# One more 2 MB home for expert weights, a late weight tile in another home, value weights loaded later, and copies shared by two engines

## The reference

```
block 1:  h = rmsnorm(x);  proj = h @ w_in                        # ten projections
          y_a = bidirectional gated linear attention (8 heads of 128), group norm, gate
          y_b = gelu(u) * spatial mix(layernorm(gelu(v))) * silu(g)
          x = rmsnorm(x + (sig(ma) * (y_a @ pa) + sig(mb) * (y_b @ pb)) @ w_out)
block 2:  pool mixer + sparse attention (8 heads of 64; an index with 8 heads, rotary turned,
          scores all keys and the 256 best are kept)               # "mid" and "sparse attention"
          x = x + cross attention to 256 memory tokens, 4 heads of 128
          x = x + mixture of 32 experts (1024 -> 256 -> 1024), two chosen per token
```

## Time and profile before

| | us |
|---|---|
| median of 3 runs (1450.04 to 1450.48) | 1450.24 |
| the profiled execution | 1448.69 |
| its span | 1446.8 |
| TensorE busy in it | 1366.7 (94%) |
| VectorE, ScalarE, GpSimd busy | 850.2, 426.3, 186.0 |
| bytes moved | 249.56 MB, mean 172 GB/s |

### The profile page before, as it was taken

One profiled execution on the slowest core, in us unless ns is written; L12 is line 12 of the kernel. 1 busy time (PEld: TensorE's weight loads), 2 busy tenths in 40 slices (PEclk: granted clock), 3 DMA queues, 4 the chain that ended last, 5 costly groups with the idle time before them and its releaser, 6 DMA issues. The chain is left out here.

```text
span 1446.8 us, 16453 instructions
## 1 busy us (share of the span) xinstructions
PE 1366.7 (94%) x5920; PEld 891.8 (62%) x5920; DVE 850.2 (59%) x1661; ACT 426.3 (29%) x718; POOL 186.0 (13%) x246
## 2 busy tenths in 40 slices
PE   7999999999999899999999999999899798999876
PEld 3577686887887668888887434445485445333322
DVE  5587787888888747877476459745573414222111
ACT  2434444544454215101112233133312421000000
POOL 0120212222210100000000026200000001222221
PEclk9999999999999999999999999999999999999999
DMA  8574657778752443222233333011213658999997
GB/s 322 124 175 154 130 134 179 167 182 188 169 133 78 90 159 129 87 106 88 102 131 117 88 91 106 22 51 46 88 58 137 257 190 320 400 407 404 413 407 272
DMA packets 65009, 249.56 MB, mean 172 GB/s; under 512 B 10464, under 2 KB 12128, under 8 KB 58144
## 3 DMA queue, kind: packets, MB, share of 16 engines
q1 hardware_dynamic: 43232, 207.57, 38.7%
q0 software_dynamic: 19008, 34.62, 13.3%
q10 hardware_dynamic: 2688, 6.29, 1.1%
HBM read 228.13 MB, written 12.58 MB: 166 GB/s over the span
## 5 line engine op out<-in xcount | busy, mean ns | idle before, releaser
L3474 PE MATMUL moe_banks<-weight_slots,moe_room 128*64 128x512 f32 x400 | 93.4, 617 | 10.3 <-DMA weight_slots<-in_w_gu 7.8
L659 PE MATMUL gla_proj<-hT,weight_slots 128*128 128x512 f32 x224 | 98.4, 593 | 1.9 <-DVE hT L1155 1.9
L2219 PE MATMUL mid_p_proj<-hT,weight_slots 128*128 128x512 f32 x208 | 92.1, 595 | 1.8 <-PEq L226 1.8
L3631 DVE SCALAR_TENSOR_TENSOR moe_room<-moe_banks,moe_kept,moe_room 128x256 f32<-128x256 f32 x16 | 7.7, 484 | 130.3 <-ACT moe_room L3586 130.3
L589 PE MATMUL gla_proj<-hT,weight_slots 128*128 128x256 f32 x320 | 77.2, 381 | 0.0
L844 ACT ACTIVATE gla_level_decay<-gla_level_decay 128x1024 f32<-128x1024 f32 x56 | 59.2, 1058 | 51.8 <-DVE gla_level_decay L1024 51.1
L659 PEld LDWEIGHTS gla_proj<-hT,weight_slots 128*128 128x128 f32 x224 | 41.6, 190 | 50.6 <-issue 49.8
L2219 PEld LDWEIGHTS mid_p_proj<-hT,weight_slots 128*128 128x128 f32 x208 | 39.0, 190 | 51.7 <-issue 51.6
L3474 PEld LDWEIGHTS moe_banks<-weight_slots,moe_room 128*64 128x64 f32 x400 | 29.8, 141 | 65.8 <-issue 54.7
L589 PEld LDWEIGHTS gla_proj<-hT,weight_slots 128*128 128x128 f32 x320 | 59.7, 192 | 10.5 <-issue 3.3
L589 PE MATMUL gla_proj<-weight_slots 128*128 128x256 f32 x272 | 64.6, 380 | 0.6 <-ACT weight_slots L790 0.6
(11 more groups left out here) (540 smaller groups left out, 2907.2 us busy)
## 6 DMA issues: line engine op xcount, KB each, us to landing
weight_slots<-in_w_gu SPq DMA_DIRECT2D x25, 2048.0 KB, 23.7
weight_slots<-in_w_gla SPq DMA_DIRECT2D x40, 512.0 KB, 4.2
weight_slots<-in_w_dn SPq DMA_DIRECT2D x10, 2048.0 KB, 34.7
weight_slots<-in_w_merge SPq DMA_DIRECT2D x32, 512.0 KB, 4.7
gla_w_sums<-in_w_gla SPq DMA_DIRECT2D x42, 256.0 KB, 4.7
gla_w_sums<-weight_slots POOLq DMA_DIRECT2D x40, 256.0 KB, 4.1
weight_slots<-in_w_out SPq DMA_DIRECT2D x16, 512.0 KB, 4.4
gla_w_sums<-in_w_gla POOLq DMA_DIRECT2D x28, 256.0 KB, 6.4
```

The costliest lines, as they stand in the source:

```text
L659: last = nc.tensor.matmul(pj[:, n % 2, :], lhsT, rhs, start=(k == 0), stop=(k == KT - 1))
L2219: last = nc.tensor.matmul(pw[:, n % 2, :], a, b, start=(k == 0), stop=(k == KT - 1))
L3474: last = nc.tensor.matmul(pG[rows, e, :], hgT[:, k, rows], core.as_gate_up(at[k // 4])[:, x, k % 4, :], start=(k == 0), stop=(k == KT - 1))
L3631: nc.vector.scalar_tensor_tensor(out=hid[:, e], in0=pG[:, e, FF:2 * FF], scalar=rs2[:, e, 1:2], in1=sa[:, e], op0=ALU.mult, op1=ALU.mult). ...
```

## The change

It has four parts. `PLACES` becomes 12, with a new 2 MB tensor `weight_slots_5` (`W5`) as home 11; part 11 is issued in the cross stage behind part 9. To fit, `rs_final` is allocated with the tensors that end with the mixers. The pair `(FILL, 5)` gets slots 11 and 3, and its second tile is issued after `("y", (QG, 7))`. In the mid stage the turned copy of the last index query is issued before the value weights, and the separate wait for the projection goes, as the copy's own wait covers it. In the cross stage ScalarE copies bank 0 and VectorE bank 1, each with its own semaphore, and the value product waits for each half by itself.

```diff
-PAIR_SLOTS = [(9, 10)] * 5 + [(11, 4)]
+PAIR_SLOTS = [(9, 10)] * 5 + [(11, 3)]
...
-PLACES = 11
+PLACES = 12
...
-        return (self.W3[:], quarters(self.xT), quarters(self.hT), self.W4[:], quarters(self.x_rows))[i - 6]
+        return (self.W3[:], quarters(self.xT), quarters(self.hT), self.W4[:], quarters(self.x_rows), self.W5[:])[i - 6]
...
                         if j == V_ and head < HEADS:
                             load_values(head)
-                        elif j == V_:
-                            load_tile((FILL, 5), 1)
-                        else:
+                        elif j < V_:
                             load_tile((j // 2, 1), j % 2)
...
                         elif kind == "y" and m[0] == FB:
                             load_sums((FILL, 5))
+                        elif kind == "y":
+                            load_tile((FILL, 5), 1)
...
                 turn_index(3, 2)
-                sp.wait_ge(proj_done, done_by(QI + 3))
+                turn_index(4, 3)
                 sp.dma_start(wv, dram["w_v2"].rearrange("p (k c) -> p k c", c=T)).then_inc(core.w_in[0], 16)
-                turn_index(4, 3)
...
                 sp.wait_ge(zn_done, 4)
                 core.load_part(sp, 9)
+                core.load_part(sp, 11)
...
                         if h:
-                            pe.wait_ge(t_out, MB * (h - 1) + c + 1)
+                            pe.wait_ge((t_out, t_out2)[c], h)
...
                 def values(h):
-                    pe.wait_ge(t_out, MB * (h + 1))
                     if h:
                         pe.wait_ge(y_out, h)
                     for c in range(MB):
+                        pe.wait_ge((t_out, t_out2)[c], h + 1)
...
-                    for c in range(MB):
-                        act.wait_ge(t_done, MB * h + c + 1)
-                        nc.scalar.copy(prT[:, h % 2, c], pT[:, c, :]).then_inc(t_out, 1)
+                    act.wait_ge(t_done, MB * h + 1)
+                    nc.scalar.copy(prT[:, h % 2, 0], pT[:, 0, :]).then_inc(t_out, 1)
...
+                def copy_second(h):
+                    if h >= 2:
+                        dve.wait_ge(o_done, h - 1)
+                    dve.wait_ge(t_done, MB * h + 2)
+                    nc.vector.tensor_copy(prT[:, h % 2, 1], pT[:, 1, :]).then_inc(t_out2, 1)
...
                 top(1)
                 probs(1)
                 normed(3)
+                copy_second(0)
                 top(2)
                 store(0)
                 probs(2)
+                copy_second(1)
                 top(3)
                 store(1)
                 probs(3)
+                copy_second(2)
                 store(2)
+                copy_second(3)
                 store(3)
...
-        rs1 = ctx.enter_context(nc.sbuf_tensor("rs_final", [P, T], F32))
...
+        rs1 = mixer.enter_context(nc.sbuf_tensor("rs_final", [P, T], F32))
...
+            core.W5 = sb("weight_slots_5", [P, 4, KT * P])
```

More of the change, by code:

```diff
@@ L1198, in gla_stage @@
         core.w_n[j] += 16 * HEADS
-    for slot, times in zip((4, 5, 9, 10, 11), (1, 2, 6, 6, 3)):
+    for slot, times in zip((3, 5, 9, 10, 11), (1, 2, 6, 6, 3)):
         core.w_n[slot] += 16 * times
@@ L2438, in cross_stage @@
                                           "turned", "turned_out", "o_done", "y_out", "dve_chain", "act_chain"))
-        h_ready = core.sem("h_ready")
+        h_ready, t_out2 = core.sem("h_ready"), core.sem("cr_turned_out_second")
         w0 = list(core.w_n)
```

## The result

| | before | changed |
|---|---|---|
| median of the runs | 1448.73 us (9 runs) | 1437.95 us (9 runs) |
| ratio to before, 95% interval | | 0.9938 [0.9923, 0.9952] |
| the same comparison once more, another chip session | 1447.20 us | 1438.56 us, 0.9940 [0.9922, 0.9957] |
| span of the profiled execution | 1446.8 us | 1436.6 us |

0.9938 of 1448.73 is 9.0 us less (7.0 to 11.2); the prediction had 8.7 less, 1441.5 as a median. It started from 1450.24, the median of the first three runs; the ratio taken from there gives 1441.2. The changed kernel's own median, 1437.95, lies just under the lower end of the range, 1438.0, because the nine runs of the kernel before have a lower median than its first three. The spans of the two profiled executions differ by 10.2 us.

A forecast was written before the change was run, and what follows sets the result against it. TensorE's pace bounds the early stages, the expert-weight bytes left when transfer engines fill bound the last hundred microseconds; -5.2 - 1.6 - 2.3 + 0.4 = -8.7 us, from 1450.24 to 1441.5 us, range 1438.0 to 1445.0.

The forecast's parts named there:

- The home, -5.2: Expert stage: one 2 MB weight load moved forward to the cross stage saves 5.2 us while transfer engines are full.
- the slower rival: Cross and routing stages: the moved load delays the router's weights, giving a time over 1450.2 us; chance 0.04.
- The rival of a partial return: Expert stage: gathers take the freed room or hold pairs 11 to 15; half of 5.2 us, 1444.1; chance 0.10.
- The late tile, -1.6: First mixer's last head: loading the tile earlier shortens TensorE's 3.98 us wait at 474 by 1.6 us.
- the second price: First mixer's last head: eight matmuls behind the wait take 3.26 us instead of 1.89 at 1.2 GHz, losing 1.4 us.
- the likeliest case: Whole kernel: the main forecast of 1441.5 us, with the slow clock after the last head's wait kept; chance 0.42.
- The rival with 0.25: First mixer's last head: the shorter wait also restores the clock, so 1.4 us more vanish, 1440.1 us; chance 0.25.
- counter-example: Expert pair at 1354.77: sixteen matmuls take 5.35 us instead of 3.65 after a 2.19 us wait, cited against clock recovery.
- The value weights, -2.3: Mid stage: issuing index copies before the value weights removes TensorE's wait of 2.26 us at 840.90, saving 2.3 us.
- The copies, +0.4: Cross stage: splitting each head's copies between ScalarE and VectorE costs 0.4 us; head 2 loses 0.8, head 3 gains 0.4.

The follow-up runs named there:

- part 1 alone: Only the twelfth home, with the load of part 11 issued right behind part 9, added to the kernel before: ratio 0.9958, 6.1 us gained.
- late load: Only the twelfth home added to the kernel before, used late: part 11 loaded behind part 10 in the routing stage; ratio 0.9984, 2.3 us gained.
- the kernel with two tiles: Change without the split copies, plus a second load of the late tile near 464.7 into a slot nobody reads: ratio 0.9972 to the kernel before.

## Why the prediction was right, and where it was off

**The home, -5.2:** right in mechanism and size (5.3 by the traces, 6.1 by the times of part 1 alone). The first wait moved to pair 12, pair 15 came nearer to the first pair by 5.8 us in the two profiled kernels, and the router started on time, so the slower rival is out. The rival of a partial return is out too for the early load. The late load returns only a part, but because of when it is issued; whether gathers take up freed room was not tested.

**The late tile, -1.6:** the forecast gain of 1.6 is the one term that came out wrong: it measured 3.9. The mechanism of the wait held: the late tile slowed the summing transfer, 6.8 to 4.9 us, as the second load does again. The size held as well: 1.8 us counted from the first summing transfer, 2.0 in the pair's start. (The wait left was forecast near 2.4 us and is 1.12 in the changed kernel, 1.6 in the mean of the six.) The step that failed is the second price, "the 1.4 us of slow clock", which I kept in the likeliest case: it vanished. The rival with 0.25 came true, and it was under-priced. The 1.4 us counted the pair alone, while the matmuls behind it run slow too, and a fall costs 1.6 to 2.8 us by the mid stage.

Two things misled me. I took one execution's 3.98 us for the wait of the kernel, where six have 2.92 to 4.28. And I weighed the clock by one counter-example, 5.35 us after a gap of 2.19. Here the clock was kept in all eight executions with waits of 1.11 to 3.40 us and lost in all five with 3.54 to 4.28. Among the later expert pairs the wait does not sort the cases. The same program, profiled twice, lost the clock after 1.97 us (1366.77) and kept it after 2.06:

```profile
1367.63 3.65 PE L3483 MATMUL moe_banks<-weight_slots,moe_room 128*64 128x512 f32 x16 [2.06 <-DMA weight_slots<-in_w_gu]
```

What else decides there no run shows, so the counter-example was no measure for this place. The Trainium skill (TensorE: Matmul & The Clock Gate, HAM oscillation) names long idle gaps of TensorE as what lets the clock fall and slows the matmuls behind them. By that the shorter wait should have kept the clock, as I had written. This place agrees, in six of six executions with the tile moved; the expert pairs do not.

**The value weights, -2.3:** right, 2.1 us by the traces. VectorE's operands were ready at 831.5, 4.3 us ahead of the scores. No wait for the value weights appears in TensorE's timeline of the mid stage, so moving the load cost nothing visible.

**The copies, +0.4:** right, 0.45 us. Head 2's values end 0.89 us later (forecast 0.8) and head 3 gives 0.43 back (0.4). But the working was silent on head 0, of whose 1.30 us head 1 gives 1.01 back, so the sum was luckier than its walk.

**The sum.** By the traces the terms are -5.3, -3.9, -2.1 and +0.45, -10.9 us, near the profiled difference of -10.2; the times say -9.0 (-11.2 to -7.0). The forecast of -8.7 lies in that interval, but that it comes within 0.3 us of the measured time is luck: by the traces the late tile alone is 2.3 us under-priced. The mean granted clock points the same way: 0.9908 in the 64 executions of the kernel before that were timed beside the experiments, 0.9927 in the fifteen of the changed one. Of 1445 us that is 2.7 us more of full clock, an estimate, of which the last head's 1.9 would be the larger part.

What stays open: the size of the late home's gain, where the kernel with two tiles loses its clock, and what decides over the clock among the expert pairs.

## What to carry to other kernels

Where a stage's end is set by full transfer engines, count the bytes still to come when they fill up: each buffer that lets 2 MB go earlier was worth about its transfer time, for one buffer fewer as for one more, but only in part when the load went out as the engines filled up; it pays in full if the load goes out while the engines have room. A load that nobody waits for can still cost through the transfers beside it; loading it a second time, into a place nobody reads, tests this apart from the dependence. Splitting a copy between two engines paid only in the place where the second engine was idle, and a working must cover every repetition. Whether the clock falls behind a wait has to be read in several executions, and its price from the next fixed point of the program, not from the first slow matmuls alone.

## What the runs showed of the hardware

- TensorE's granted clock in the last head: kept at 2.4 GHz in eight executions with waits of 1.11 to 3.40 us, down to 1.2 GHz in five with waits of 3.54 to 4.28. The five lose 1.6 to 2.8 us by the mid stage.
- Among the later expert pairs it fell after waits of 1.85 to 2.34 us and was kept after others of up to 2.06. A fall in the kernel before, in the windows around pair 13 (1388.52, behind a wait of 1.86 us):

```profile
1388.00:1390.00 2.00, 1.48 (x6) 0.70 (x8) 0.00 (x0) 0.00 (x0) 1.67 (x2) 0.83 1.02 434
1390.00:1392.00 2.00, 2.00 (x6) 0.61 (x4) 0.00 (x0) 0.00 (x0) 1.37 (x3) 0.50 1.01 434
```

- The same program keeps or loses 1.7 us at a place that the change doesn't touch: the first eight query matmuls of the cross stage take 3.67 or 5.37 us after the same wait of 2.07 us. Rows of both kinds:

```profile
1103.12 3.67 PE L2461 MATMUL cr_p_q<-hT,weight_slots 128*128 128x512 f32 x8 [2.07 <-PEq L1874]
```

```profile
1104.13 5.37 PE L2461 MATMUL cr_p_q<-hT,weight_slots 128*128 128x512 f32 x8 [2.07 <-PEq L1874]
```

  These are the changed kernel's two profiles, so a comparison of one trace with one trace carries such steps, and only times over many runs or stage lengths with them taken off are fair.
- The accumulating transfer of line 1134 (256 KB, from on-chip memory into on-chip memory) landed after 4.3 to 5.4 us in the six executions with no plain load issued less than 7 us ahead. With one plain load of 512 KB issued 1.7 to 2.8 us ahead it took 6.0 to 7.0 us in five of six, and 6.8 where that load was a second copy. The sixth (home used late) has it issued 6 us behind the load, and there it took 3.5 us.
